# Opening that mixes unmodulated tokens, a first projection unit in plain fp32, and a ring of three modulation pieces

## The reference, cut to what matters

```python
def rms_norm(x, g):
    y = xf * lax.rsqrt(jnp.mean(xf * xf, axis=-1, keepdims=True) + RMS_EPS)
    return (y * g).astype(x.dtype)
# mod = silu(c) @ mod_w[l] + mod_b[l]      6 * 1024 values per layer and side
# h   = rms_norm(x) * (1 + scale) + shift  the modulated tokens
def centred_shift(h):
    prev = jnp.pad(h[:, :-1], ((0, 0), (1, 0), (0, 0)))
    nxt = jnp.pad(h[:, 1:], ((0, 0), (0, 1), (0, 0)))
    return 0.5 * (prev + nxt) - h
# features
    xx = centred_shift(h)
    xr, xw, xk, xv, xa = (h + xx * mu[i] for i in range(5))
    r = _heads(xr @ wr); k = _heads(xk @ wk); v = _heads(xv @ wv)
    # tanh(xw @ w1), xa @ a1, sigmoid((h + xx * mu[5]) @ g1): the low-rank inputs
```

## Time and profile before

| what | us |
|---|---|
| median of 3 runs | 2160.78 |
| lowest and highest run | 2155.02, 2161.09 |
| the profiled execution, its own time | 2155.79 |
| its span, first to last instruction | 2154.0 |
| PE busy in the span | 2011.3 (93%) |
| DVE, ACT, POOL busy | 1179.6, 831.6, 371.2 |
| mean granted TensorE clock | 0.965 |

### The profile page before, as it was taken

The page is one execution under the profiler, slowest core; times in us unless marked ns, Lnnn a source line. Parts: engine busy times, 40 slices in busy tenths (PEclk is TensorE's granted clock), DMA queues, the critical chain, the costliest instruction groups (busy, mean ns, idle before and its releaser), DMA issues. The chain is left out here.

```text
span 2154.0 us, 52861 instructions
## 1 busy us (share of the span) xinstructions
PE 2011.3 (93%) x22567; PEld 1764.5 (82%) x22567; DVE 1179.6 (55%) x1945; ACT 831.6 (39%) x1435; POOL 371.2 (17%) x399
## 2 busy tenths in 40 slices
PE   5799998899999998699999999999999899999998
PEld 4688886688887887599999999999875477888887
DVE  3865535566666665347767576666365424333333
ACT  2433324455555543235323232334335424422221
POOL 0000000566666663030000000003210010000000
PEclk8799998799999999899999999999999999999999
DMA  9577775001111000430221221211120023333332
GB/s 317 179 230 233 224 242 160 22 21 36 36 36 36 19 12 11 165 98 10 89 79 59 70 81 56 87 62 59 61 77 1 2 77 88 97 104 92 97 106 79
DMA packets 224957, 194.31 MB, mean 90 GB/s; under 512 B 13274, under 2 KB 208356, under 8 KB 224228
## 3 DMA queue, kind: packets, MB, share of 16 engines
q1 hardware_dynamic: 224740, 191.13, 28.3%
HBM read 170.66 MB, written 17.83 MB: 88 GB/s over the span
## 5 line engine op out<-in xcount | busy, mean ns | idle before, releaser
L722 DVE TENSOR_TENSOR ffn_lo<-ffn_raw,ffn_hi 128x1024 fp32r<-128x1024 f32 (+1 forms) x58 | 77.5, 1335 | 196.2 <-ACT ffn_hi L717 196.2
L742 PE MATMUL banks<-operand_hi,ffn_w_hi 128*128 128x384 f32 x464 | 156.4, 337 | 0.7 <-DVE ffn_w_lo L3234 0.7
L742 PE MATMUL banks<-operand_lo,ffn_w_hi 128*128 128x384 f32 x464 | 155.9, 336 | 0.0
L742 PE MATMUL banks<-operand_hi,ffn_w_lo 128*128 128x384 f32 x464 | 155.8, 336 | 0.0
L742 PE MATMUL banks<-mix_hi,proj_hi 128*128 128x386 f32 (+1 forms) x384 | 136.7, 356 | 15.2 <-DVE proj_lo L915 10.1
L742 PE MATMUL banks<-operand_hi,ffn_hi 128*128 128x512 f32 x352 | 138.6, 394 | 5.4 <-DVE operand_lo L519 3.1
L717 ACT CAST ffn_hi<-ffn_raw 128x1024 fp32r<-128x1024 f32 (+1 forms) x60 | 68.3, 1139 | 184.4 <-PE banks L742 182.9
L742 PE MATMUL banks<-operand_lo,ffn_hi 128*128 128x512 f32 x352 | 138.1, 392 | 0.0
L742 PE MATMUL banks<-operand_hi,ffn_lo 128*128 128x512 f32 x352 | 137.9, 392 | 0.0
L742 PE MATMUL banks<-mix_hi,proj_lo 128*128 128x386 f32 (+1 forms) x384 | 131.9, 343 | 0.0
L742 PE MATMUL banks<-mix_lo,proj_hi 128*128 128x386 f32 (+1 forms) x384 | 131.8, 343 | 0.0
(11 more groups left out here) (337 smaller groups left out, 5742.9 us busy)
## 6 DMA issues: line engine op xcount, KB each, us to landing
mod_raw<-in_mod_w SPq DMA_DIRECT2D x96, 512.0 KB, 5.3
ffn_raw<-in_ff_w SPq DMA_DIRECT2D x32, 1024.0 KB, 5.2
ffn_raw<-in_ff_w SPq DMA_DIRECT2D x46, 512.0 KB, 3.8
ffn_raw<-in_ff_w SPq DMA_DIRECT2D x16, 704.0 KB, 4.5
proj_raw<-in_rw_wr SPq DMA_DIRECT2D x16, 256.0 KB, 6.1
proj_raw<-in_rw_wk SPq DMA_DIRECT2D x16, 256.0 KB, 6.2
proj_raw<-in_rw_wv SPq DMA_DIRECT2D x16, 256.0 KB, 5.9
rwkv_out_raw<-in_rw_wo SPq DMA_DIRECT2D x8, 512.0 KB, 4.6
```

Of the source, the lines that this page charges most:

```text
L722: signal(eng, eng.tensor_tensor(self.lo[s][:, 0:k_tiles, :], self.raw[s][:, 0:k_tiles, :], self.hi[s][:, 0:k_tiles, :].bitcast(F32), ALU.s ...
L742: mm = pe.matmul(out, a, b, start=(first and n == 0), stop=(last and n == 2), skip_group_check=onto)
```

## The change

In the opening, nothing waits for the modulation any more but the modulation's own steps. The turned tokens leave PSUM as they are (scaled, not modulated) into `normed`; neighbour sums and the first mix are made there, on unmodulated tokens, in a new tile `mix_unshifted` (`pre`). The blocks 8 and 9 of the modulation are no longer computed in the opening. The first three weight parts are loaded in the opening, and SP no longer waits for the write of `residual`; ACT does, later (`c.spilled`). Behind the barrier the mix is modulated in place (a gain and a shift per side, `fill`) and corrected at the four edge columns, where a neighbour is missing (`first_edges`). Unit 0 then multiplies raw weights with this mix as plain fp32 matmuls, two for a k in place of six. The split of that mix into hi and lo, which units 1 to 7 need, is made beside and behind it: lo overwrites the mix (`mix_lo0` has its place), so a piece waits for unit 0's product of that k. `normed` and `shifted` themselves are modulated by ACT, a tile per unit, in units 0 to 7 (`modulate`, `edges`). The ring of the modulation has three pieces in place of two, 40 blocks in place of 38 are left to the units, and `mods_of` gives unit 0 none. Raw tokens also leave PSUM in fewer, wider copies, and the scaling by the root is shared between DVE (4 tiles) and ACT (2).

```diff
-MOD_EARLY = 10
-MOD_SHARE = 13
+MOD_EARLY = 8
+MOD_SHARE = 14
-MOD_DEEP, MOD_PARTS = 2, 2
+MOD_DEEP, MOD_PARTS = 3, 2
@@ opening, SP: last lines
+                for part in range(3):
+                    n, k = part // 2, CT // 2 * (part % 2)
+                    sp.dma_start(first_weights[part][:], wr[:, k:k + CT // 2, n * P:n * P + P]).then_inc(c.first_weights[part], 16)
-                sp.wait_ge(raw_copied, 2 * CT)
+                sp.wait_ge(raw_copied, 4 + CT)
                 sp.dma_start(spilled, h[:]).then_inc(c.spilled, 16)
-                sp.wait_ge(c.spilled, 16)
@@ opening, DVE
+                for k in range(CT):
+                    dve.wait_ge(xs_copied, k + 1)
+                    signal(dve, v.tensor_tensor(xx[:, k, :], a[:, k, 0:PAD], a[:, k, 2:PAD + 2], ALU.add), sums, k + 1)
+                    dve.wait_ge(kept, k + 1)
+                    v.scalar_tensor_tensor(pre[:, k, :], xx[:, k, :], c.par[:, PHALF + k:PHALF + k + 1], pre[:, k, :],
+                                           ALU.mult, ALU.add).then_inc(premixed, 1)
                 mods.store(dve, 0)
@@ rwkv_inputs
-            count, steps = MOD_BLOCKS - MOD_EARLY, CT * (UNITS - 1)
-            places = [(2 * b + 1) * steps // (2 * count) for b in range(count)]
+            count, steps = MOD_BLOCKS - MOD_EARLY, CT * (UNITS - 2)
+            places = [CT + (2 * b + 1) * steps // (2 * count) for b in range(count)]
@@ SP
-                        need(sp, w_rest, w_at + part - 2 if part > 2 else 0)
+                        if part < 5:
+                            sp.wait_ge(w_product, used(part - 3))
+                        else:
+                            sp.wait_ge(w_rest, split(part - 3))
-                load(0)
-                load(1)
-                load(2)
                 load_low(0)
-                load_mods(0)
+                load_mods(1)
                 for n in range(UNITS):
                     load(2 * n + 3)
                     load(2 * n + 4)
-                    load_mods(n + 1)
+                    if n:
+                        load_mods(n + 1)
@@ PE
+                def first_unit():
+                    for k in range(CT):
+                        part, j = k // HALF_K, k % HALF_K
+                        if j == 0:
+                            pe.wait_ge(w_loaded[part], 16)
+                        pe.wait_ge(mixed, k + 1)
+                        for b, (at, width) in enumerate(PAD_BLOCKS):
+                            mm = pe.matmul(c.bank[b][:, 0:width], w_raw[part][:, j, :], pre[:, k, at:at + width],
+                                           start=(k == 0), stop=(k == CT - 1))
+                        mm.then_inc(w_product, 1)
+                first_unit()
+                for n in range(1, UNITS):
@@ ACT, per unit n < 8, on shifted and normed, in two sides each
+                def modulate(k):
+                    for r, cols in SIDES:
+                        nc.scalar.activation(xx[:, k, cols], xx[:, k, cols], ACT.Identity, scale=c.gain[:, 0, 0, r, k:k + 1])
```

More of the change, by code:

```diff
@@ L147, in __init__ @@
         self.tiles = CT // parts
-        self.raw = [sb(f"raw{s}", [P, self.tiles, MOD_W]) for s in range(deep)]
+        self.raw = [sb(f"raw{s}", [P, self.tiles, MOD_W]) for s in range(deep - len(placed))] + list(placed)
         self.row = sb("row", [P, MOD_W])
@@ L383, in _ @@
                     mods.gain(v, 0, 0, PNM, r).then_inc(gains, 1)
-                dve.wait_ge(gains, 2)
-                for k in range(CT):
-                    dve.wait_ge(s_turned, k + 1)
-                    v.tensor_scalar(a[:, k, CTX + 2:TOK + 2], scaled_bank(k)[1][:, 0:LAT], c.gain[:, 0, 0, 0, k:k + 1],
-                                    c.mod[:, 0, k, 0:1], ALU.mult, ALU.add).then_inc(a_lat, 1)
-                mods.store(dve, 1)
             @block.scalar
@@ L743, in three_passes, with rwkv_inputs @@
     return mm
-def rwkv_inputs(c, d, a, xx, hidden, full, dram, mods_before):
+def rwkv_inputs(c, d, a, xx, pre, mix_lo0, w_raw, hidden, full, mod_raw, dram, mods_before):
     nc = c.nc
@@ L776, in rwkv_inputs @@
             "low_loaded", "low_rounded", "low_rest", "low_mix_rest", "low_product"))
-        factored, kept_part = sem("mix_factors"), sem("own_part")
+        edges_made, filled, filled_odd, modulated, edged = (sem(n) for n in (
+            "edges_made", "first_mix_shifted", "first_mix_shifted_odd", "normed", "normed_edges"))
         small_copied = sem("hidden_copied")
@@ L809, in mixed_low, with split, used @@
             return CT + min(n + 1, 2 * CT) + sum(len(low_steps(u)) for u in range(n)) + nth
-        def column(t, k):
-            return t[:, k, :]
+        def split(part):
+            return part - 1
+        def used(part):
+            return HALF_K * (part + 1) if part < 2 else part + 7
         with nc.Block() as block:
@@ L930, in mix, with first_edges, edges @@
+                def first_edges(k):
+                    if k % 2:
+                        dve.wait_ge(filled_odd, k // 2 + 1)
+                    at_edges(pre[:, k, :], first_edge, k).then_inc(mixed, 1)
+                def edges(k):
+                    dve.wait_ge(modulated, k + 1)
+                    signal(dve, at_edges(xx[:, k, :], edge, k), edged, k + 1)
                 def mix(out_, mu, k, done):
@@ L971, in _ @@
                     if n < CT:
-                        shift(i)
+                        shift(n + 1)
+                        edges(n)
                     if m < 2:
@@ L975, in _ @@
                     for nth, (step, _) in enumerate(low_steps(n)):
-                        mix(full[1][:], MU_LOW[step // CT], step % CT, mixed_low(n, nth) + 1)
+                        need(dve, low_product, step)
+                        mix(low_whole[:], MU_LOW[step // CT], step % CT, mixed_low(n, nth) + 1)
                         if m < 2 and nth == 0:
```

290 lines of the change are left out of this document (166 added, 124 removed).

## The result

| | median, us | runs | profiled execution | its span | granted clock |
|---|---|---|---|---|---|
| before | 2157.91 | 2155.02 to 2161.09 (4) | 2155.8 | 2154.0 | 0.965 |
| after | 2137.89 | 2135.57 to 2138.77 (4) | 2137.34 | 2135.6 | 0.971 |

The ratio is 0.9912, 95% interval 0.9886 to 0.9938. The kernel is faster, as forecast, by 20.0 us where 13.3 were forecast.

The account below looks back on a forecast made before the run. The start was held bound by a chain (modulation, modulated tokens, barrier, mix, split), then PE. Terms -15.4 - 8.4 + 6.6 + 3.2 + 0.7 = -13.3 us on 2155.8 gave 2142.5, median forecast 2147, range 2139 to 2157.

Parts of the forecast that it names:

- start of unit 0: Opening up to the first projection unit: it begins at 46.3 us, 15.4 us sooner, bounds 45.2 to 48.0.
- unit 0 and handover: First unit's fp32 matmuls and the split until unit 1 begins: 14.7 us in place of 23.1, 8.4 us less.
- unit 1: Second projection unit: 17.8 us in place of 11.2, 6.6 us more, with stalls of 4.3 and 1.8 us.
- unit 2 to the end of the projections: Remaining projection units: 3.2 us more for extra modulation blocks and 0.7 us allowed for their closer succession.
- everything behind: All work after the projections: no change was counted in the sum.
- DVE's chain: Opening: sums and mixes of 8 tiles end at 42.8 us, later than the modulation's possible store at about 41.7.
- The ring's gap: Opening: the ring of eight pieces is empty for a moment as piece 8 waits for the first multiplication, 0.7 us.
- The new wait: Unit 1: PE stalls 4.3 us for weight part 3, which SP issues only behind the fourth modulation piece.
- The wait of 1.8 us for the low-rank step: Unit 1: the first low-rank step's chain, behind the late weight part, makes PE wait 1.8 us more.
- the closer spacing: From unit 2 on: modulation blocks follow every 5.9 us, before every 6.3; 0.7 us allowed, 0 to 4.
- The rival in which the ring becomes the bound: Projection units: each of 38 blocks waits 0.9 us for pieces, 34 us in all, giving 2181; chance 5%.
- the gain is partly given back later: Recurrence and what follows: own waits or other clocks give 6 us back, 2153; chance 10%.

Follow-up runs that it names:

- The version with its blocks in PE's gap: Changed kernel with weight parts 3 and 4 issued before unit 1's fourth modulation piece, and blocks 0 and 1 multiplied behind the parameter rows: 2130.13 us, again 2137.53.
- the ring of two: Changed kernel with two modulation ring pieces in place of three: 2151.94 us, ratio 0.9999 to the kernel before.
- the experiment with SP's order: Changed kernel with SP issuing weight parts 3 and 4 ahead of unit 1's fourth modulation piece: 2133.46 us, ratio 0.9916 to the kernel before.
- again: The kernel before, unedited, run and profiled a second time: 2159.12 us, ratio 1.0002 to the kernel before beside it.
- 2nd: The changed kernel, unedited, run and profiled a second time: 2135.56 us, ratio 0.9922 to the kernel before.
- 3rd: The changed kernel, unedited, run and profiled a third time, on one chip with the kernel before: 2142.78 us, ratio 0.9932.
- 4th: The changed kernel, unedited, run and profiled a fourth time: 2142.66 us, ratio 0.9923 to the kernel before.
- the idle DVE work: Changed kernel with nine clears of a spare 128x512 tile on DVE ahead of the barrier: 2141.81 us, ratio 0.9958 to the kernel before.

## Why the prediction was right or wrong

| step | forecast | measured, first profiles |
|---|---|---|
| start of unit 0 | 46.3 (-15.4) | 49.35 (-12.3) |
| unit 0 and handover | 14.7 (-8.4) | 15.1 (-8.0) |
| unit 1 | 17.8 (+6.6) | 19.5 (+8.3) |
| unit 2 to the end of the projections | +3.9 | +0.8 |
| sum there | -13.3 | -11.2 |
| everything behind | 0 | -7.2 |

**The start.** That DVE's chain would be last was wrong, in all four profiles of the changed kernel: the store waited 1.6 to 2.5 us for the fold. The ring's gap, priced at 0.7 us, made the other chain last. The first buffer now comes free only when block 0 is multiplied behind the scaled tiles, and from 24 to 30 us the transfers ran at 115 in place of 351 GB/s: 6 x (351 - 115) / 351 = 4.0 us of transfer lost, and the last piece was multiplied 4.6 us later than before. The store, forecast at 41.7, was at 46.31. The version with its blocks in PE's gap had the last piece at 39.02 and the fold at 40.31, against 39.05 and 40.18 in the kernel before, so all of this was the order of the multiplications. DVE's chain itself ended at 44.5 where I had 42.8, because its reciprocal was 0.9 us later and the first mix another 0.8; the pairs took 2.1 us each, as forecast. The barrier gave 1.0 back: DVE waited 0.73 in it, not 1.7.

**Unit 0** has the right length by luck. The forecast added PE's work (10.8 and 2.1 us) and a tail of 1.8 us, and called DVE and ACT no bound. PE's part was forecast well: 12.70 us for 32 records. But what ended the term was DVE. From 49.12 it modulated tiles and corrected edges, waited 1.14 us for ACT's last tile, and from 55.76 on it made all eight lo parts without a pause, PE having finished each product before DVE came to it. The twelve profiles of the changed kernel and its variants settle it: PE's 32 records took 12.16 to 13.52 us, and in ten of them unit 1 began 15.08 to 15.12 us behind unit 0 all the same. Only in the two where PE took 13.5 was it 15.35 and 15.51. So, up to some 13.3 us of PE's work, neither the clock nor the passes of fp32 set this term; where PE was faster it waited longer (12.16 us and then 2.94 with the ring of two). The clock was granted at 0.50 from 50 to 52 us and at 1.00 from 54 to 56, 1.2 and 2.4 GHz, as the forecast had it. A split first unit on unmodulated tokens wasn't tried, so what fp32 alone is worth stays open.

**Unit 1.** The new wait is shown: 4.54 us for 4.3, part 3 issued behind the fourth piece at 68.92, and it goes when the order is changed. Hi of part 3 began at 73.20, 4.3 us after the issue; the forecast, from the landings in the earlier trace rows, had 3.9. The Trainium skill (DMA: Bandwidth & Descriptors, Anatomy of one DMA) has a fit, measured on DMAs that GpSimd issues, which gives an estimate of 3.8 us for piece and part in a row. SP issues these, the piece at 68.51, and 4.7 us lie from there to hi, so rule and rows were both low. The wait of 1.8 us for the low-rank step was not seen, since PE ran at half clock right then (0.50 from 76 to 78) and reached that step later. Where PE was faster, in the experiment with SP's order, it is there with 1.4. The half clock behind the gap stood in the forecast only as a bound. The term was 1.7 us too small.

**Steady state.** Three blocks more (3.2) and the closer spacing (0.7) gave +3.9; +0.8 was measured. The ring of two shows the third buffer's worth at this spacing, 10.9 us. The forecast took it as a means against loss and never asked what it takes away: PE's idle time over the whole stretch fell from 4.7 us (of 260.2) to 3.6 (of 261.0), and its waits for pieces from 1.6 to 0.6. That is 1 of the 3.1 us; where the other 2 went isn't shown. The rival in which the ring becomes the bound was wrong for this kernel; it is what the kernel with two buffers does at a smaller price, 8.1 us of waits in place of the rival's 34.

**The step that failed** is the last one of the sum: an execution's rest taken as fixed, and the rival "the gain is partly given back later" written with one sign only. Up to the end of the projections the forecast missed by 2.1 us; behind it 7.2 us came that I had at 0, and it is these that put the time below the range. In three later groups the medians of before and after differ by 15.3, 15.0 and 16.3 us. The profiles give 12.1 to 13.0 of that up to the end of the projections (356.25 less 344.1, 343.7 and 343.2), so about 3 are left behind it. The four runs of each kernel in the first comparison gave 20.0; its interval, 13.4 to 24.6 us, holds the 15.5 that the three later ones have in the mean. So of the 7.2 us some 3 repeat and some 4 are how the first two executions happened to run: the rest of an unedited program was 1797.8 and 1804.6 (before) and 1786.5 to 1799.7 (after). The 3 are a difference of medians whose intervals reach 3 to 5 us to either side in each group, so they are no sharp number.

The traces show a place where the two kernels differ each time. The rest can be cut where SP issues loads and stores, which are the same in all of them. In us:

| stretch | before | again | after | 2nd | 3rd | 4th |
|---|---|---|---|---|---|---|
| keep table to the second load of `k_pair` | 76.7 | 77.4 | 76.7 | 74.4 | 76.0 | 75.5 |
| from there to the recurrence's first store (`mixed_all`) | 69.4 | 71.7 | 64.9 | 66.2 | 66.6 | 65.8 |
| to the load of the output projection's weights | 388.0 | 391.5 | 389.7 | 387.6 | 395.4 | 392.8 |
| to the load of attention's `wv` | 564.1 | 564.4 | 560.9 | 559.9 | 562.7 | 564.2 |
| to the end | 699.6 | 699.6 | 698.5 | 698.4 | 699.1 | 699.5 |

In the second row the kernel before is 2.9 to 6.8 us longer, and the eight profiles of the variants are all like those of after (65.0 to 66.2). The last 17.6 us of it, in both profiles of before, are 13.9 to 14.2 in all twelve others, and the difference is the clock: 0.81 there and 1.00 in the twelve. Before, before again, and after:

```profile
484.68:502.30 17.62, 17.18 (x394) 13.93 (x392) 10.22 (x20) 7.83 (x15) 8.09 (x11) 0.81 0.09 25
487.79:505.41 17.62, 17.19 (x394) 13.95 (x392) 10.20 (x20) 7.83 (x15) 8.09 (x11) 0.81 0.10 25
472.63:486.56 13.93, 13.93 (x394) 11.79 (x392) 9.99 (x20) 7.85 (x15) 8.13 (x11) 1.00 0.12 33
```

That is 3.4 to 3.7 us at the same 394 matmuls, which is the size of what repeats. Why the clock fell there only in the kernel before stays open. The start alone doesn't explain it: with the ring of two the projections ended at 354.4, 1.8 us sooner than before, and the clock stayed at 1.00. The ring of two lost these microseconds again further on, so how much of them reaches the end isn't settled either. The last row gives another 0.7 us in the mean.

The first feed-forward part varies between executions of the changed kernel too (fourth row). The dip shown above, in the profile before, from 970 to 990 us is in its second profile too (0.83 over the same work, 977 to 997), in the fourth of after (0.82 and 0.83), in part in the third, and not in the first two. The first pair's 7.2 us are 4.5 from the second row, 3.2 from the fourth, 1.1 from the last and 1.7 lost in the third. The recurrence behind its first store varies most, by 8 us among the four profiles of after. Against a general dependence on when the recurrence starts speaks the idle DVE work: the projections ended 9.0 us later, and the rest was not longer.

Against those 15.5 us the forecast of 13.3 was 2.2 us off, but in two misses that partly cancel: 0.3 to 1.2 us too much up to the end of the projections, and the 3 behind it at nothing. The range was placed on one execution and its gap to a median of three runs.

## What to carry to other kernels

When an edit moves the first use of a prefetch ring later, work out from the row of the transfers how long the queue has nothing to load; that gap moves the last piece by about as much (4.0 us of transfer lost, 4.6 us of delay; without the gap the delay was gone). Where a queue issues in order, look at each wait for a free buffer and at what stands behind it: another order of the issues took a wait of 4.5 us away. Where one term's length is the same in every variant though the engine it was blamed on takes more or less time, another engine sets it, as DVE did in unit 0. And before a prediction is placed by one profiled execution, ask how much the untouched part differs between executions and chips, and read the clock over the same work and not at the same time: here the rest differed by 18 us over 14 profiles, more than the effect that was asked for.

## What the runs showed of the hardware

- What lies behind the projections took 1786.5 to 1804.6 us in the six profiles of the two unedited kernels. The medians of the kernel before were 2157.79 and 2158.93 in the last two groups of runs, on one chip, and 2153.45 and 2150.88 on two others. Only ratios within a group compare.
- Behind PE's wait of 4.5 us the granted clock was 0.50 though PE was then fed without a gap (76 to 78 us above). In the experiment with SP's order PE waited 1.38 us inside unit 1 in place of 4.54, and unit 1 took 15.1 us in place of 19.5: 3.2 us less of waiting brought 4.4. So the wait in the middle of the matmul stream cost more than its length here.
- In the recurrence both profiles of the kernel before had a granted clock of 0.81 over 17.6 us, and all twelve of the changed kernel and its variants 1.00 over the same 394 matmuls in 13.9 to 14.2 us. All the edited work lies more than 120 us ahead of that place; what moved the clock isn't shown.
- With more asked of DMA (244 GB/s against 223), weight parts landed sooner in the median and modulation pieces later; SP's order and the ring had changed too, so the load alone isn't shown as the cause. For pieces (in `mod_raw`), then parts, of the changed kernel, 84 to 345 us, against the earlier trace rows:

```profile
DMA to landing us min/median/max: 3.6/5.5/8.2
...
DMA to landing us min/median/max: 3.3/5.2/6.3
```
